# A decoder step in float32 on one core: the place of one low-part step in VectorE's order, in the odd tile of each pair

## Chip, cores and metric

One core of one Trainium2 chip runs the whole program in a single launch. The metric is the device time of one execution in microseconds (us); for the kernel before, the median of three runs is given. Profiles come from one execution that the hardware profiler recorded.

## What is computed

One layer of a hybrid decoder for two request groups that share the weights: 1024 prompt tokens and 8 x 4 sample tokens, 1056 in all, with a model width of 1024. The layer is a half-step feed-forward block, a mixer (sparse attention in three branches beside a pooling mixer) and a second half-step feed-forward block. The change lies in the feed-forward block, which the program runs twice:

```python
D_MODEL = 1024
D_FF = 2816

def swiglu_ffn(x, g, w_gate, w_up, w_down):
    h = rmsnorm(x, g)
    return (jax.nn.silu(h @ w_gate) * (h @ w_up)) @ w_down

...
        xp = xp + 0.5 * swiglu_ffn(xp, *ffn1)
        xs = xs + 0.5 * swiglu_ffn(xs, *ffn1)
        ...
        xp = xp + 0.5 * swiglu_ffn(xp, *ffn2)
        xs = xs + 0.5 * swiglu_ffn(xs, *ffn2)
```

## The kernel before

**Tiles and stages.** Each feed-forward block is one stage, `stage_ffn` (stages `f1` and `f2`; the mixer's stages lie between them). The tokens lie along the free dimension, cut into three thirds (chunks 0, 1 and 2) of 352 columns. The 2816 hidden channels are cut into 22 tiles `g` of 128 channels, and two tiles make one of 11 pairs `q`; the even tile comes first, the odd tile second. For each tile TensorE computes gate and up (`tile`), and behind the odd tile of a pair it computes the pair's down products: 24 of them, 8 blocks of output channels for each of the three thirds. `order_of(q)` says which third comes first: (1, 0, 2) in all pairs but the last of a stage, which has (0, 1, 2).

**High and low parts.** A float32 operand is split into a rounded high part and the low part that is left, and a product is three matmuls (`product3`, L110 to L114): high by high, high by low, low by high. ScalarE makes the high parts (`high_w` of the weights, L502; `high_a` of the activation, L529), VectorE the low parts (`low_w`, L630; `low_a`, L663). `a_hi` and `a_lo` hold the activation's parts for the two tiles of a pair.

**Gate and up.** A tile takes eight weight forms 0 to 7. Some are loaded halves (`gu_raw`), some are sums of halves that VectorE makes (`sum_w`, L626), as the first two thirds are computed in a Strassen-like form; the third third is computed plainly. VectorE puts the banks together (`base`, `above`, `fifth`, `far`), multiplies by the row norm (`rescale`, L654, after ScalarE's Silu, L523) and by up (`activate`, L659). The product for a third lies in `gate_of[c]`, that is `near`, `far`, `third` for c = 0, 1, 2 (`third` shows as `in_var` or `f_var` in the trace). `activate(g, c)` is followed by ScalarE's `high_a(g, c)` and then VectorE's `low_a(g, c)`, which raises `a_ready[c]`.

**Order.** Each engine's order is written out by hand, and semaphores hold the engines together. At the end of a tile VectorE runs, from `rescale(g, 1)` on (L751 to L768): the second third's product; next weights 1 (low part) and 2 (sum); the sum for the first third's up (waits for event 10, TensorE's form 7 of the first two thirds); the first third's product; the second third's low part; next weights 2 and 3; the last third's product (waits for event 11, the end of the tile on TensorE); the first third's low part; next weights 3; the last third's low part. Then come the 24 updates of the trunk (`update`, L669). ScalarE runs at the same time: next weights 0, `high_a(g, 1)`, next weights 1 and 2, `high_a(g, 0)`, next weights 3, `high_a(g, 2)` (L577 to L586).

**Down products.** TensorE waits for `a_ready[c]` at the first product of each third (L890). The products go round four banks (`down_bank`): product n of a pair goes to bank n % 4, and from n = 4 on it waits until update n - 4 has read that bank (`down_free`, L892). A product is six matmuls: two tiles of the pair, three each. `update` n waits for product n and adds half of it to the trunk.

**Loads.** SP loads the next tiles' weights in halves (`load_half`); each waits for a count of `w_lo_done`, that is for low parts of the weights that VectorE has made.

Of the kernel before, what the change touches and what calls it, by code (L numbers as in the profile page):

```python
# [116 lines left out]
def chunk(c):  # L117
    return slice(c * CH, (c + 1) * CH)
# [200 lines left out]
def stage_ffn(nc, mem, K, xT, gain, w_gate, w_up, w_down, name, b_sum, copies=(), copied=None,  # L319
# [17 lines left out]
    with ExitStack() as scope:  # L337
# [86 lines left out]
        def event(g, e):  # L424
            return EVENTS * g + e
# [11 lines left out]
        with nc.Block() as block:  # L437
# [174 lines left out]
            def _(dve):  # L612
                def sum_w(v, i):
                    gate_1, gate_2, up_1, up_2 = gu_raw[:, 0, 0:KH], gu_raw[:, 0, KH:KT], gu_raw[:, 1, 0:KH], gu_raw[:, 1, KH:KT]
                    at, count = SUM_OF[i]
                    if i != 1:
                        dve.wait_ge(raw_landed[0][i == 5], 16 * v + 16)
                    if i in (1, 2):
                        dve.wait_ge(raw_landed[1][0], 16 * v + 16)
                    if i == 1:  # L620
                        dve.wait_ge(raw_landed[1][1], 16 * v + 16)
                    if i in (3, 5):
                        dve.wait_ge(w_summed, 4 * v + count - 1)
                    a, b, op = {1: (up_1, up_2, ALU.add), 2: (up_1, gate_1, ALU.subtract),
                                3: (w_sum[:, 0], gate_1, ALU.subtract), 5: (gate_2, w_sum[:, 0], ALU.subtract)}[i]
                    dve.tensor_tensor(w_sum[:, at], a, b, op).then_inc(w_summed, 1)  # L626

                def low_w(v, i):
                    dve.wait_ge(w_hi_done, 8 * v + i + 1)
                    dve.tensor_tensor(w_lo[:, i % 4], form(i), w_hi[:, i % 4].bitcast(F32),  # L630
                                      ALU.subtract).then_inc(w_lo_done, 1)
# [20 lines left out]
                def rescale(g, c):  # L652
                    dve.wait_ge(silu_done[c], g + 1)
                    dve.tensor_tensor(gate_of[c], gate_of[c], inv[:, chunk(c)], ALU.mult).then_inc(silu_scaled[c], 1)  # L654

                def activate(g, c, up, ready, count):
                    dve.wait_ge(silu_scaled[c], g + 1)
                    dve.wait_ge(ready, count)
                    dve.tensor_tensor(gate_of[c], gate_of[c], up, ALU.mult).then_inc(act_done[c], 1)  # L659

                def low_a(g, c):
                    dve.wait_ge(a_hi_done[c], g + 1)
                    dve.tensor_tensor(a_lo[:, g % 2, chunk(c)], gate_of[c], a_hi[:, g % 2, chunk(c)].bitcast(F32),  # L663
                                      ALU.subtract).then_inc(a_ready[c], 1)

                def update(q, n):
                    c, m = order_of(q)[n // KT], n % KT
                    dve.wait_ge(down_done, DOWNS * q + n + 1)
                    dve.scalar_tensor_tensor(xT[:, m, chunk(c)], down_bank[n % 4], 0.5, xT[:, m, chunk(c)],  # L669
                                             ALU.mult, ALU.add).then_inc(down_free, 1)  # L670
                    return c, m
# [35 lines left out]
                for q in range(PAIRS):  # L707
                    for g in (2 * q, 2 * q + 1):
                        more = g + 1 < FT
                        sum_w(g, 5)  # L710
                        low_w(g, 4)
                        low_w(g, 5)
                        low_w(g, 6)
                        if g == 0:
                            norm.mean_square(dve, sum_bank, 2)
                        dve.wait_ge(product_done, event(g, 5))
                        dve.wait_ge(first_copied, g + 1)
                        dve.tensor_tensor(base, base, bank_6, ALU.add).then_inc(base_done, 1)
                        dve.wait_ge(base_done, g + 1)
                        dve.tensor_tensor(above, base, bank_7, ALU.add).then_inc(above_done, 1)  # L720
                        low_w(g, 7)
                        if g == 0:
                            dve.wait_ge(above_done, 1)
                            norm.tmp = far
                            norm.invert(dve, 2)
                        dve.wait_ge(above_done, g + 1)
                        dve.wait_ge(fifth_copied, g + 1)
                        dve.tensor_tensor(fifth, above, fifth, ALU.add).then_inc(up_far_done, 1)
                        dve.wait_ge(product_done, event(g, 6))
                        if g:  # L730
                            dve.wait_ge(a_ready[0], g)
                        dve.tensor_tensor(near, bank_1, inv[:, chunk(0)], ALU.mult).then_inc(gate_scaled[0], 1)
                        dve.wait_ge(product_done, event(g, 7))
                        if g:
                            dve.wait_ge(a_ready[2], g)
                        dve.tensor_tensor(third, bank_gate, inv[:, chunk(2)], ALU.mult).then_inc(gate_scaled[2], 1)
                        if g % 2 == 0:
                            dve.wait_ge(wd_hi_done, q + 1)
                            dve.tensor_tensor(wd_lo, wd_raw, wd_hi[:].bitcast(F32), ALU.subtract).then_inc(wd_split, 1)  # L739
                        rescale(g, 0)  # L740
                        rescale(g, 2)
                        dve.wait_ge(product_done, event(g, 8))
                        if g:
                            dve.wait_ge(a_ready[1], g)
                        dve.tensor_tensor(far, base, bank_5, ALU.add).then_inc(far_summed, 1)
                        dve.wait_ge(far_summed, g + 1)
                        dve.tensor_tensor(far, far, inv[:, chunk(1)], ALU.mult).then_inc(gate_scaled[1], 1)
                        if more:
                            sum_w(g + 1, 1)
                            low_w(g + 1, 0)  # L750
                        rescale(g, 1)  # L751
                        activate(g, 1, fifth, up_far_done, g + 1)
                        if more:
                            low_w(g + 1, 1)
                            sum_w(g + 1, 2)
                        dve.wait_ge(product_done, event(g, 10))
                        dve.wait_ge(far_summed, g + 1)
                        dve.tensor_tensor(base, base, bank_7, ALU.add).then_inc(up_near_done, 1)
                        activate(g, 0, base, up_near_done, g + 1)
                        low_a(g, 1)  # L760
                        if more:
                            low_w(g + 1, 2)
                            sum_w(g + 1, 3)
                        activate(g, 2, bank_up, product_done, event(g, 11))
                        low_a(g, 0)
                        if more:
                            low_w(g + 1, 3)
                        low_a(g, 2)  # L768
                    if q:
                        dve.wait_ge(down_free, DOWNS * q)  # L770
                    for n in range(DOWNS):
                        c, m = update(q, n)
                        if q < PAIRS - 1:
                            continue
                        if ahead:
                            if c == 1:
                                next_norm.low(dve, xT, h_hi, h_lo, 0, range(m, m + 1))
                            if c == 2 and m < LOWS_AHEAD:
                                next_norm.low(dve, xT, h_hi, h_lo, 1, range(m, m + 1))
                            if (c, m) == (2, 0):  # L780
                                next_norm.fold(dve, 0)
                            if (c, m) == (2, 5):
                                next_norm.mean_square(dve, bank_5, 0)
                        if finish:
                            if (c, m) in SQUARED_BEHIND:
                                fin.mean_square(dve, SQUARED_BEHIND[(c, m)])
                            if (c, m) in NORMED_BEHIND:
                                if (c, m) == (1, 4):
                                    dve.wait_ge(fin.gain_in, 16)
                                fin.invert_and_left(dve, NORMED_BEHIND[(c, m)])  # L790
# [2498 lines left out]
```

## Time and profile before

| | us |
|---|---|
| median of 3 runs | 2894.51 |
| lowest and highest run | 2894.26, 2901.41 |
| profiled execution | 2893.93 |
| its span, first to last instruction | 2892.3 |

In that span the stage `f1` takes about 791 us (458 to 1249) and `f2` about 777 us (2097 to 2874). How to read the rows below: times are us from the start of the span unless marked ns. PE is TensorE's matmuls, DVE is VectorE, ACT is ScalarE, L112 is line 112 of the kernel. A matmul's recorded length overlaps the next one's, so the pace of matmuls is read from start to start. The same holds for VectorE and ScalarE when they run back to back. The note in brackets at the end of a row is the idle time of that engine just before, and what ended it; "issue" means that the engine waited for nothing that the profile shows. PEclk is the clock that TensorE was granted as a share of 2.4 GHz: 1.00 is that, 0.50 is 1.2 GHz.

### The profile page before, as it was taken

What the parts mean: (1) busy time and instruction counts of PE and PEld (TensorE: products, weight loads), DVE (VectorE), ACT (ScalarE), POOL (GpSimd) and SP (SyncE); (2) the same over time, 40 slices, a digit from 0 to 9 for tenths busy, and PEclk for the clock granted to TensorE, in tenths of its full rate; (3) what the DMA queues carried; (4) which work ended last, traced back from release to release, by engine and by line L of the source; (5) the groups of instructions that cost most, each with busy time, mean ns of one, the idle gap of its engine ahead of it and who ended that gap; (6) DMA issues with size and microseconds to landing.
All of it is one profiled execution on the core that took longest, in us unless ns stands there. A gap on an engine that the chain in (4) does not pass through costs nothing. (4 is left out here: it accounts for less than half of the span.)

```text
span 2892.3 us, 44546 instructions
## 1 busy us (share of the span) xinstructions
PE 2597.1 (90%) x17112; PEld 2437.7 (84%) x17112; DVE 1761.2 (61%) x3447; ACT 1111.7 (38%) x2099; POOL 384.7 (13%) x427
## 2 busy tenths in 40 slices
PE   4999986999999999999988888677979999999997
PEld 4898885999999999988976666456879999999997
DVE  5444446766666666664147768555386666666666
ACT  4656555222222222232346656434152222222223
POOL 4444430000000000000002222451000000000001
PEclk9999998999999999999979979999999999999999
DMA  4131311311111111031311010586011111111111
GB/s 179 63 124 63 124 61 46 106 48 45 44 45 55 48 44 44 30 113 43 100 62 45 23 45 34 178 286 220 30 30 45 44 45 44 48 59 48 52 45 68
DMA packets 173315, 207.93 MB, mean 72 GB/s; under 512 B 16750, under 2 KB 154863, under 8 KB 170410
## 3 DMA queue, kind: packets, MB, share of 16 engines
q1 hardware_dynamic: 162434, 144.91, 15.9%
q0 software_dynamic: 10672, 60.19, 5.6%
q8 instruction: 137, 2.24, 0.3%
q14 instruction: 72, 0.59, 0.1%
HBM read 191.39 MB, written 18.01 MB: 72 GB/s over the span
## 5 line engine op out<-in xcount | busy, mean ns | idle before, releaser
L669 DVE SCALAR_TENSOR_TENSOR trunk<-f_bank,trunk 128x352 f32<-128x352 f32 x528 | 272.7, 523 | 198.0 <-PE f_bank L114 198.0
L112 PE MATMUL f_bank<-f_a_hi,f_wd_hi 128*128 128x352 f32 x1056 | 347.0, 329 | 44.7 <-issue 40.4
L113 PE MATMUL f_bank<-f_a_lo,f_wd_hi 128*128 128x352 f32 x1056 | 345.1, 327 | 0.0
L114 PE MATMUL f_bank<-f_a_hi,f_wd_lo 128*128 128x352 f32 x1056 | 344.4, 326 | 0.0
L112 PE MATMUL cs_sum<-cs_x_hi,cs_w_hi 128*128 128x256 f32 (+1 forms) x768 | 231.1, 301 | 32.4 <-DVE cs_x_lo L1379 22.1
L112 PEld LDWEIGHTS f_bank<-f_a_hi,f_wd_hi 128*128 128x128 f32 x1056 | 201.7, 191 | 50.4 <-issue 50.3
L112 PE MATMUL f_bank<-f_s_hi,f_w_hi 128*128 128x352 f32 x704 | 228.0, 324 | 0.0
L114 PE MATMUL f_bank<-f_s_hi,f_w_lo 128*128 128x352 f32 x704 | 227.4, 323 | 0.0
L113 PE MATMUL f_bank<-f_s_lo,f_w_hi 128*128 128x352 f32 x704 | 226.3, 321 | 0.0
L114 PE MATMUL cs_sum<-cs_x_hi,cs_w_lo 128*128 128x256 f32 (+1 forms) x768 | 218.6, 285 | 0.0
L113 PE MATMUL cs_sum<-cs_x_lo,cs_w_hi 128*128 128x256 f32 (+1 forms) x768 | 218.4, 284 | 0.0
L114 PEld LDWEIGHTS f_bank<-f_a_hi,f_wd_lo 128*128 128x128 f32 x1056 | 203.0, 192 | 0.0
L1236 POOL TENSOR_TENSOR cs_x_lo<-cs_x,cs_x_hi 128x516 fp32r<-128x516 f32 x128 | 171.0, 1336 | 234.8 <-ACT cs_x_hi L1293 234.8
L113 PEld LDWEIGHTS f_bank<-f_a_lo,f_wd_hi 128*128 128x128 f32 x1056 | 201.9, 191 | 0.1
L560 ACT ACTIVATE f_base<-f_bank 128x352 f32<-128x352 f32 x44 | 20.0, 453 | 472.7 <-PE f_bank L114 472.7
L630 DVE TENSOR_TENSOR f_w_lo<-f_gu_raw,f_w_hi 128x512 fp32r<-128x512 f32 x176 | 121.1, 688 | 119.4 <-ACT f_w_hi L502 119.1
L112 PE MATMUL f_bank<-f_h_hi,f_w_hi 128*128 128x352 f32 x528 | 171.7, 325 | 20.0 <-DVE f_h_lo L644 15.5
L112 PEld LDWEIGHTS cs_sum<-cs_x_hi,cs_w_hi 128*128 128x128 f32 x768 | 147.6, 192 | 43.1 <-DVE cs_x_lo L1379 40.3
L112 PE MATMUL f_bank<-in_h_hi,f_w_hi 128*128 128x352 f32 x528 | 171.1, 324 | 6.5 <-DVE f_w_lo L630 4.9
L114 PE MATMUL f_bank<-f_h_hi,f_w_lo 128*128 128x352 f32 x528 | 171.4, 325 | 0.0
L630 DVE TENSOR_TENSOR f_w_lo<-f_w_sum,f_w_hi 128x512 fp32r<-128x512 f32 x176 | 121.1, 688 | 82.5 <-ACT f_w_hi L502 80.2
L113 PE MATMUL f_bank<-f_h_lo,f_w_hi 128*128 128x352 f32 x528 | 171.3, 324 | 0.0
(447 smaller groups left out, 6859.7 us busy)
## 6 DMA issues: line engine op xcount, KB each, us to landing
f_gu_raw<-in_w_ffn_gate_dram SPq DMA_DIRECT2D x88, 256.0 KB, 3.0
f_gu_raw<-in_w_ffn_up_dram SPq DMA_DIRECT2D x88, 256.0 KB, 3.0
as_pages<-in_cache_kv_slc_dram SPq DMA_DIRECT2D x128, 128.0 KB, 4.0
as_pages<-in_cache_kv_slc_dram POOLq DMA_DIRECT2D x128, 128.0 KB, 4.2
at_spread<-saved_rows SPq DMA_DIRECT2D x16, 768.0 KB, 4.1
in_w_raw<-in_w_ffn_down_dram SPq DMA_DIRECT2D x11, 1024.0 KB, 5.0
f_wd_raw<-in_w_ffn_down_dram SPq DMA_DIRECT2D x11, 1024.0 KB, 5.0
x_saved<-trunk SPq DMA_DIRECT2D x2, 2112.0 KB, 13.8
```

The costliest lines, as they stand in the source:

```text
L112: pe.matmul(out, w_hi, x_hi, start=first, stop=False, skip_group_check=onto)
L113: pe.matmul(out, w_hi, x_lo, start=False, stop=False, skip_group_check=onto)
L114: return pe.matmul(out, w_lo, x_hi, start=False, stop=last, skip_group_check=onto)
L560: act.activation(base, bank_1, ACT.Copy).then_inc(first_copied, 1)
L630: dve.tensor_tensor(w_lo[:, i % 4], form(i), w_hi[:, i % 4].bitcast(F32), ALU.subtract).then_inc(w_lo_done, 1)
L669: dve.scalar_tensor_tensor(xT[:, m, chunk(c)], down_bank[n % 4], 0.5, xT[:, m, chunk(c)], ALU.mult, ALU.add).then_inc(down_free, 1)
L1236: pool.tensor_tensor(x_lo[s][:, 0:ODD], x[s][:, 0:ODD], x_hi[s][:, 0:ODD].bitcast(F32), ALU.subtract).then_inc(diff_lo_done, 1)
```

## The change

`low_a(g, 1)`, VectorE's low part of the second third's activation, is moved in odd tiles: from behind the first third's product to directly behind the second third's product, ahead of the next weights' low part 1, the sum 2, the sum for the first third's up and the first third's product. In even tiles it stays where it was. No instruction is added or taken out, and the other engines' programs are the same.

```diff
                         rescale(g, 1)
                         activate(g, 1, fifth, up_far_done, g + 1)
+                        if g % 2:
+                            low_a(g, 1)
                         if more:
                             low_w(g + 1, 1)
                             sum_w(g + 1, 2)
@@
                         activate(g, 0, base, up_near_done, g + 1)
-                        low_a(g, 1)
+                        if g % 2 == 0:
+                            low_a(g, 1)
                         if more:
                             low_w(g + 1, 2)
```

## Rows read from the trace of the kernel before

**Rows 1.** The page: TensorE's busy time, share and instructions.
```profile
PE 2597.1 (90%) x17112; PEld 2437.7 (84%) x17112; DVE 1761.2 (61%) x3447; ACT 1111.7 (38%) x2099; POOL 384.7 (13%) x427
```

**Rows 2.** Groups of TensorE's instructions: count, busy, mean ns, idle before and releasers.
```profile
L112 PE MATMUL f_bank<-f_a_hi,f_wd_hi 128*128 128x352 f32 x1056 | 347.0, 329 | 44.7 <-issue 40.4 <-DVE f_a_lo L663 4.3
```

**Rows 3.** Time line of TensorE, a pair's end near 676: start, length, instruction.
```profile
676.00 0.32 PE L114 MATMUL f_bank<-f_s_hi,f_w_lo 128*128 128x352 f32 x1
678.40 0.40 PE L112 MATMUL f_bank<-f_a_hi,f_wd_hi 128*128 128x352 f32 x1 [2.07 <-issue]
678.64 0.32 PE L113 MATMUL f_bank<-f_a_lo,f_wd_hi 128*128 128x352 f32 x1
...
682.33 0.32 PE L112 MATMUL f_bank<-f_a_hi,f_wd_hi 128*128 128x352 f32 x1
682.49 0.32 PE L113 MATMUL f_bank<-f_a_lo,f_wd_hi 128*128 128x352 f32 x1
```

**Rows 4.** Time line of VectorE there, and of the pair near 812.
```profile
673.89 0.53 DVE L659 TENSOR_TENSOR f_far<-f_far,f_fifth 128x352 f32<-128x352 f32 x1
675.50 0.69 DVE L630 TENSOR_TENSOR f_w_lo<-f_w_sum,f_w_hi 128x512 fp32r<-128x512 f32 x1 [1.08 <-ACT f_w_hi L502]
...
677.77 0.52 DVE L663 TENSOR_TENSOR f_a_lo<-f_far,f_a_hi 128x352 fp32r<-128x352 f32 x1
678.21 0.69 DVE L630 TENSOR_TENSOR f_w_lo<-f_w_sum,f_w_hi 128x512 fp32r<-128x512 f32 x1
...
681.32 1.81 DVE L669 SCALAR_TENSOR_TENSOR trunk<-f_bank,trunk 128x352 f32<-128x352 f32 x4
...
809.63 0.53 DVE L659 TENSOR_TENSOR f_far<-f_far,f_fifth 128x352 f32<-128x352 f32 x1
...
817.05 0.52 DVE L669 SCALAR_TENSOR_TENSOR trunk<-f_bank,trunk 128x352 f32<-128x352 f32 x1
```

**Rows 5.** Time line of ScalarE at the pair's end near 676.
```profile
674.45 0.50 ACT L529 ACTIVATE f_a_hi<-f_far 128x352 fp32r<-128x352 f32 x1 [1.75 <-DVE f_far L659]
674.86 0.61 ACT L502 ACTIVATE f_w_hi<-f_w_sum 128x512 fp32r<-128x512 f32 x1
...
679.53 0.63 ACT L502 ACTIVATE f_w_hi<-f_w_sum 128x512 fp32r<-128x512 f32 x1 [1.14 <-DVE f_w_sum L626]
```

**Rows 6.** Stretches behind waits: length, busy PE, PEld, DVE, ACT, POOL, PEclk, DMA.
```profile
541.20:543.20 2.00, 2.00 (x7) 2.00 (x8) 2.00 (x5) 0.95 (x2) 0.00 (x0) 0.50 0.00 0
...
2640.50:2642.50 2.00, 2.00 (x7) 2.00 (x8) 2.00 (x5) 0.98 (x2) 0.00 (x0) 0.50 0.00 0
...
678.40:680.40 2.00, 2.00 (x13) 2.00 (x13) 2.00 (x5) 0.87 (x2) 0.00 (x0) 1.00 0.02 4
...
2105.20:2107.00 1.80, 1.77 (x11) 1.80 (x12) 1.80 (x5) 0.00 (x0) 0.00 (x0) 1.00 0.00 0
...
517.50:519.50 2.00, 1.92 (x12) 1.92 (x13) 0.99 (x3) 0.94 (x2) 0.00 (x0) 1.00 0.91 293
...
1223.50:1225.50 2.00, 2.00 (x13) 2.00 (x14) 1.01 (x2) 0.00 (x0) 0.00 (x0) 1.00 0.00 0
```

**Rows 7.** Time line of TensorE, pair near 812: first and fifth down product.
```profile
814.13 0.59 PE L112 MATMUL f_bank<-f_a_hi,f_wd_hi 128*128 128x352 f32 x1 [2.07 <-issue]
...
819.61 0.32 PE L112 MATMUL f_bank<-f_a_hi,f_wd_hi 128*128 128x352 f32 x1
```

**Rows 8.** Time line of TensorE: first matmuls behind three shorter waits.
```profile
2105.23 0.40 PE L112 MATMUL f_bank<-f_h_hi,f_w_hi 128*128 128x352 f32 x1 [1.78 <-DVE f_h_lo L644]
...
517.58 0.43 PE L112 MATMUL f_bank<-in_h_hi,f_w_hi 128*128 128x352 f32 x1 [1.41 <-DVE f_w_lo L630]
...
1223.44 0.40 PE L112 MATMUL f_bank<-f_a_hi,f_wd_hi 128*128 128x352 f32 x1 [1.16 <-issue]
```

**Rows 9.** Time line of VectorE at the end of the first stage's last pair.
```profile
1220.39 0.52 DVE L758 TENSOR_TENSOR f_base<-f_base,f_bank 128x352 f32<-128x352 f32 x1 [1.14 <-PE f_bank L114]
...
1222.38 0.52 DVE L659 TENSOR_TENSOR in_var<-in_var,f_bank 128x352 f32<-128x352 f32 x1 [0.41 <-PE f_bank L114]
```

## The prediction

> **What bounds the kernel now.** I read the busy line of the page first, then the groups of TensorE's instructions, then the time lines of TensorE, VectorE and ScalarE around the end of one odd tile, and last the granted clock behind each of TensorE's waits. TensorE is busy for 90% of the span [rows 1]: whatever delays it in the two feed-forward stages delays the end. The stages are almost gapless but for one place. The group of the down products' first matmuls has 44.7 us of idle time before it, 40.4 us of that in 20 waits and 4.3 us in two more [rows 2]. That is one wait at the head of each of the 22 pairs of tiles. The 40.4 us bear the name "issue", so what ends them has to be found in the time lines.
>
> I take the pair that ends near 676 us. TensorE begins the tile's last matmul at 676.00 and the first down matmul at 678.40, with 2.07 us idle; it could have begun at 676.16, since matmuls follow each other by 0.16 there (682.33 and 682.49) [rows 3]. What does it wait for? In this pair the down products begin with the second third of the tokens, and need its low part. VectorE makes that from 677.77 to 678.29 [rows 4], and TensorE starts 0.11 us later. The other 19 pairs of this order look alike: 44.7 less the two last pairs' 1.16 [rows 8] leaves 2.12 us for each of the 20. The high part from which this low part is made had been ready since 674.45 + 0.50 = 674.95 [rows 5]; between stand two steps on the next tile's weights and two on the first third.
>
> **The change, part by part.** It takes one instruction out of its place and puts it four instructions earlier, in odd tiles alone. Nothing is added: the 0.52 us step stays, its wait on the high part moves with it, it issues no DMA, and no queue of SP or POOL is passed.
>
> *The new place.* VectorE ends the second third's product at 673.89 + 0.53 = 674.42, and then idles 1.08 us, until ScalarE hands it the next weights' high part: the next low part starts at 675.50 [rows 4], 0.03 us behind the end of ScalarE's step (674.86 + 0.61) [rows 5]. ScalarE makes the activation's high part before that, so the moved step can start at 674.95 + 0.03 = 674.98. Back to back, VectorE's starts are 0.44 us apart for a step of this size (677.77 to 678.21) [rows 4]. It is thus out of the way at 675.42, 0.08 us ahead of the step behind it. What is queued behind the moved wait is that weights' step and the whole tail; by these rows none of it is delayed. Cost at the new place: nothing, because an idle slot covers it. If the slot did not hold, the tail would start up to 0.44 us later.
>
> *The old place.* The tail behind it, from 678.21 to the first update at 681.32, has no idle time [rows 4], so it moves up by 0.44: the first update starts at 680.88. ScalarE's next weights' step in the tail idles until VectorE's sum releases it (679.53) [rows 5] and moves with it, and so does the next weights' load on SP, which waits for a low part there and is not awaited until a tile later.
>
> *Where the stall goes.* The second third's low part is there at 675.5, so TensorE runs on from 676.16 into the down products. But these have four banks, and the fifth product has to wait until VectorE's first update has emptied the first bank. Four products are 24 matmuls, 24 x 0.16 = 3.9 us: TensorE arrives at the fifth at 680.02 and the bank is not free. It starts at 680.88 + 0.52 (the update) + 0.11 (the delay seen at 678.40) = 681.51. Before, the fifth product started at 682.33 [rows 3], when its bank had been free since 681.32 + 0.52 + 0.11 = 681.95 (0.52 is the update's time at 817.05 [rows 4]). The gain is 0.82 us; the restart costs 0.08 of it, since the second matmul after a wait comes 0.24 us behind the first and not 0.16 [rows 3]. **0.74 us in a plain pair**: most of the 2.07 us is not gained but moved four products down, where some 1.3 us of idle time remains (last matmul ends about 680.18, next begins 681.51).
>
> *The clock.* In six of the 20 pairs the granted clock is about 0.5 (1.2 GHz) behind the wait, in the others 1.00 (2.4 GHz) ([rows 6]: the first and the last of the six, and one of the 14). What TensorE did before was the same: a full-speed tile and then this wait. The price: 819.61 - 814.13 = 5.48 us from the first to the fifth product [rows 7] against 682.33 - 678.40 = 3.93 [rows 3], so 1.55 us. Shorter waits have rows at the full clock behind them: 1.78, 1.41 and, in a last pair, 1.16 us [rows 6, 8]. The new wait of 1.3 us is nearest to these, so I take no fall, and keep a fall in six of 20 as the other end. In such a pair the fifth product goes from 819.61 to 817.05 - 0.44 + 0.63 = 817.24 [rows 4, 7], less 0.08: **2.29 us**.
>
> *The last pairs.* Each stage's last pair begins its down products with the first third, behind a 1.16 us wait ([rows 8] has the first stage's). There VectorE's product of the last third waits for TensorE until 1222.38, and the sum before it does so at 1220.39 [rows 9]. The moved step needs 0.03 + 0.50 + 0.03 + 0.44 = 1.00 us of the 1.14 us of idle time ahead of that sum; both waits still end with TensorE. Nothing is gained or lost.
>
> *The sum.* 14 x 0.74 + 6 x 2.29 = 10.4 + 13.7 = 24.1 us, all of it on TensorE's path. The profiled execution took 2893.93 us (span 2892.3 and 1.6 around it), the median of the runs is 0.58 above it: 2894.51 - 24.1 = **2870.4 us**.
>
> **The rivals.**
>
> *The clock still falls as often.* The wait at the fifth product comes after only 3.9 us of matmuls, and no row shows a bank wait here. Six falls at 1.55 take 9.3 us of the 24.1: 2894.5 - 14.8 = 2879.7. Against it stand the waits of 1.16 to 1.78 us without a fall.
>
> *Slower: the clock falls at the new wait in every pair.* It costs 1.55 in each of the 14 plain pairs against a gain of 0.74, and leaves 2.29 - 1.55 in the six: 14 x 0.81 - 6 x 0.74 = +6.9 us, 2901.4. It decides from the sixteenth of the 20 pairs (24.1 / 1.55 = 15.5). For it: six pairs fall already with the same wait ahead of them; against it: the 14 others don't, with a longer wait than the new one. The Trainium skill ("TensorE: Matmul & The Clock Gate", section "A second HAM failure mode: psum-queue depth-cycling") speaks for this case: a kernel that cycles through PSUM banks idles briefly between groups so often that its clock goes back and forth, and pays for that between bursts. By that rule the time would be the 2901.4; the rows so far bear it out for waits of 2.06 us and more, and for none below.
>
> *The slot does not hold.* If the step in its new place pushes the tail back by its whole 0.44 us, the first update stays at 681.32, and each of the 20 pairs loses 0.44: 24.1 - 8.8 = 15.3, 2879.2. For it: only 0.08 us of slot is left over. Against it: the sequence repeats closely, 7.42 us from this product to the first update in the pair at 812 and 7.43 in that at 676 [rows 4]. The Trainium skill (same page, section "Architectural detail: the array is 16× 32×32, not 1× 128×128") calls VectorE a strict FIFO, so a wait put ahead holds all that is behind it; the trace agrees (the weights' step at 675.50 idles for ScalarE with ready work behind it), and this rival is what that would cost.
>
> *It doesn't remove the wait.* If what ends the 2.07 us is not the low part, the time is about 2894.5. For it: the view says "issue". Against: two of the 22 waits are put down to this low part by name [rows 2], and 0.11 us lies between its end and the start.
>
> **How the numbers follow.** Forecast 2870.4: 0.72. Clock falls as before, 2879.7: 0.12. Slot lost, 2879.2: 0.08. Wait stays, 2894.5: 0.04. Slower, 2901.4: 0.04. The forecast's own range: the delay may be 0.08 instead of 0.11, the shift 0.52 instead of 0.44 and the restart free, together 0.19 x 20 = 3.8 us below; a few falls of the clock lie above. Range 2867 to 2881, which takes in the two middle rivals. About 0.3% (8.7 us) is what a measurement of this kernel can tell from no change. The first three cases are all beyond it, faster 0.92; the wait that stays and most of the slower case are within it, 0.06; slower by more needs falls and a lost slot at once, 0.02.
>
> **What would show it.** In the changed profile the idle time ahead of the group of down matmuls should fall from 44.7 to about 29 us (20 x 1.33 + 2 x 1.16), and move from the first to the fifth product. The low part should run in the slot ahead of the weights' step, which should keep its distance of 1.61 us from the second third's product, and the first update should come 6.98 and not 7.42 us behind that product. The clock should stand at 1.00 behind all 20 waits. The prediction is wrong if a new wait stands elsewhere, if the fifth product comes 8.06 us or more behind the second third's product (slot lost; 681.51 - 673.89 = 7.62 is forecast), or if rows at 0.5 of the clock remain.

## The result and the profile after

| | before | after |
|---|---|---|
| median, us | 2897.39 (4 runs, 2894.26 to 2901.41) | 2870.30 (4 runs, 2866.82 to 2873.65) |
| ratio after / before | | 0.9906, 95% interval 0.9886 to 0.9926 |
| profiled execution, us | 2893.93 | 2871.22 |
| its span, us | 2892.3 | 2869.6 |

The median of before is that of the runs made beside the changed kernel. The profiled executions differ by 22.7 us; 24.1 were forecast.

The first view is again the groups of TensorE's instructions (count, busy us, mean ns, idle us before, releasers), the group of the down products' first matmuls:

```profile
L112 PE MATMUL f_bank<-f_a_hi,f_wd_hi 128*128 128x352 f32 x1056 | 343.5, 325 | 28.2 <-DVE trunk L669 25.9 <-issue 2.3
```

Against [rows 2] the idle time went from 44.7 to 28.2 us, and it has another releaser: 25.9 us of it ends with the trunk's update, not with "issue" or the low part. The 2.3 us are the two last pairs, as before. TensorE's time line at the end of the same pair (start, length, instruction, idle time before it) shows where the wait now stands:

```profile
672.07 0.33 PE L114 MATMUL f_bank<-f_s_hi,f_w_lo 128*128 128x352 f32 x1
672.23 0.33 PE L112 MATMUL f_bank<-f_a_hi,f_wd_hi 128*128 128x352 f32 x1
...
675.93 0.32 PE L114 MATMUL f_bank<-f_a_hi,f_wd_lo 128*128 128x352 f32 x1
677.52 0.43 PE L112 MATMUL f_bank<-f_a_hi,f_wd_hi 128*128 128x352 f32 x1 [1.27 <-DVE trunk L669]
677.78 0.32 PE L113 MATMUL f_bank<-f_a_lo,f_wd_hi 128*128 128x352 f32 x1
```

The first down matmul follows the tile's last by 0.16 us: the wait of [rows 3] is gone. Four products later stands the new one, 1.27 us. VectorE's time line of that stretch:

```profile
669.96 0.53 DVE L659 TENSOR_TENSOR f_far<-f_far,f_fifth 128x352 f32<-128x352 f32 x1
671.05 0.53 DVE L663 TENSOR_TENSOR f_a_lo<-f_far,f_a_hi 128x352 fp32r<-128x352 f32 x1 [0.57 <-ACT f_a_hi L529]
671.57 0.69 DVE L630 TENSOR_TENSOR f_w_lo<-f_w_sum,f_w_hi 128x512 fp32r<-128x512 f32 x1
...
676.95 2.36 DVE L669 SCALAR_TENSOR_TENSOR trunk<-f_bank,trunk 128x352 f32<-128x352 f32 x5
```

The low part sits in the old idle slot; the weights' step behind it still comes 1.61 us after the second third's product (671.57 - 669.96; 675.50 - 673.89 in [rows 4]). The first update comes 6.99 us after that product, where it came 7.43.

Last the clock behind the new waits (stretch, length, busy us of PE, PEld, DVE, ACT, POOL, then PEclk, DMA share, GB/s): the first of the 20, the one above and the last.

```profile
543.40:545.40 2.00, 2.00 (x13) 2.00 (x14) 1.71 (x4) 0.00 (x0) 0.00 (x0) 1.00 0.00 0
677.50:679.50 2.00, 1.98 (x12) 1.98 (x13) 1.78 (x4) 0.00 (x0) 0.00 (x0) 1.00 0.00 0
...
2757.70:2759.70 2.00, 1.96 (x12) 1.96 (x13) 1.81 (x4) 0.00 (x0) 0.00 (x0) 1.00 0.00 0
```

All 20 stand at 1.00; the six falls of [rows 6] are gone.

**Where the 22.7 us came from.** The second third's product of the odd tile can serve as a mark in each pair. Its first and last row in each of the two stages (of the changed kernel also the second), of the kernel before:

```profile
536.61 0.53 DVE L659 TENSOR_TENSOR f_far<-f_far,f_fifth 128x352 f32<-128x352 f32 x1
...
1218.72 0.53 DVE L659 TENSOR_TENSOR f_far<-f_far,f_fifth 128x352 f32<-128x352 f32 x1
...
2158.90 0.53 DVE L659 TENSOR_TENSOR f_far<-f_far,f_fifth 128x352 f32<-128x352 f32 x1
...
2839.70 0.52 DVE L659 TENSOR_TENSOR f_far<-f_far,f_fifth 128x352 f32<-128x352 f32 x1
```

and of the changed kernel:

```profile
535.78 0.53 DVE L659 TENSOR_TENSOR f_far<-f_far,f_fifth 128x352 f32<-128x352 f32 x1
...
602.87 0.53 DVE L659 TENSOR_TENSOR f_far<-f_far,f_fifth 128x352 f32<-128x352 f32 x1
...
1205.51 0.53 DVE L659 TENSOR_TENSOR f_far<-f_far,f_fifth 128x352 f32<-128x352 f32 x1
...
2148.38 0.53 DVE L659 TENSOR_TENSOR f_far<-f_far,f_fifth 128x352 f32<-128x352 f32 x1
...
2815.93 0.53 DVE L659 TENSOR_TENSOR f_far<-f_far,f_fifth 128x352 f32<-128x352 f32 x1
```

Between the marks lie ten pairs' ends per stage: 682.11 us became 669.73 in the first (-12.4), 680.80 became 667.55 in the second (-13.2). That is 25.6 us in the part that the change touches. The rest of the span gave 2.9 us back: 0.8 us were gained ahead of the first mark, 2.7 lost between the stages' marks (940.18 us became 942.87) and some 1.0 behind the last one. Both losses lie in places that the change doesn't touch, the second stage's opening and its end; the last section shows them.

### The profile page after: what moved, and what is told of

It reads as the page before. It is cut to its first block and busy times, and to the rows that moved or that the text cites. A ratio compares the mean times of both kernels' runs of the same rounds, so it can differ in the third digit from the quotient of the medians.

```text
span 2869.6 us, 44546 instructions
## 1 busy us (share of the span) xinstructions
PE 2595.8 (90%) x17112; PEld 2434.0 (85%) x17112; DVE 1764.2 (61%) x3447; ACT 1112.5 (39%) x2099; POOL 385.2 (13%) x427
## 5 line engine op out<-in xcount | busy, mean ns | idle before, releaser
L112 PE MATMUL f_bank<-f_a_hi,f_wd_hi 128*128 128x352 f32 x1056 | 343.5, 325 | 28.2 <-DVE trunk L669 25.9
L113 PE MATMUL f_bank<-in_h_lo,f_w_hi 128*128 128x352 f32 x528 | 171.0, 324 | 0.0
```

Of the source, the lines that this page charges most:

```text
L112: pe.matmul(out, w_hi, x_hi, start=first, stop=False, skip_group_check=onto)
L113: pe.matmul(out, w_hi, x_lo, start=False, stop=False, skip_group_check=onto)
```

## The experiments

The theory has three parts. The low part of the second third starts the down products; the first update, with its four banks, sets the fifth product; and the clock falls only behind long waits. The rivals: the gain comes from VectorE's shorter tail alone; the updates held the pairs all along; the falls of the clock have nothing to do with the wait; the shorter tail is worth as much in even tiles. "Ten-pair sums" below are the distances between the marks above, both stages together; they and the counts of falls come from one profiled execution of each kernel. All were timed beside the kernel before, and the gains in us are the ratio's share of its median of 2898 us.

**Low part early, but behind the slot** (`e1_halfway`, against the kernel before):

```diff
                         if more:
                             low_w(g + 1, 1)
                             sum_w(g + 1, 2)
+                        if g % 2:
+                            low_a(g, 1)
                         dve.wait_ge(product_done, event(g, 10))
...
                         activate(g, 0, base, up_near_done, g + 1)
-                        low_a(g, 1)
+                        if g % 2 == 0:
+                            low_a(g, 1)
```

> The low part of the second third stands behind next weights 2, ahead of the sum for the first third's up: early enough to let TensorE start sooner, but not in VectorE's idle slot, so the first update stays 7.43 us behind the second third's product. Theory (the low part starts the down products, the first update sets the fifth, and the clock falls only behind waits of 2.06 us and more): the wait ahead of the first product shrinks to about 1.0 us, one of 0.3 to 0.5 us stands ahead of the fifth, which starts 8.0 us behind the second third's product where it was 8.44: 20 x (0.44 - 0.11) = 6.6 us, and no falls of the clock gives 9.3 more, together about 16 us faster than the kernel before. Rival, only the shorter tail of VectorE gives the gain and the clock is chance: 0 us. Rival, the falls of the clock don't depend on the wait: about 7 us faster.

Measured: 2878.13 us, ratio 0.9933 (0.9911 to 0.9956), some 19 us faster; the ten-pair sums are 17.2 us shorter. TensorE at the first and at the fifth product of the third pair:

```profile
675.54 0.40 PE L112 MATMUL f_bank<-f_a_hi,f_wd_hi 128*128 128x352 f32 x1 [1.02 <-issue]
...
680.09 0.43 PE L112 MATMUL f_bank<-f_a_hi,f_wd_hi 128*128 128x352 f32 x1 [0.45 <-DVE trunk L669]
```

VectorE's second third's product and low part there:

```profile
672.09 0.53 DVE L659 TENSOR_TENSOR f_far<-f_far,f_fifth 128x352 f32<-128x352 f32 x1
...
674.92 0.52 DVE L663 TENSOR_TENSOR f_a_lo<-f_far,f_a_hi 128x352 fp32r<-128x352 f32 x1
```

The fifth product comes 8.00 us behind the second third's product, as forecast. The tail is as long as before, yet the gain is there: the early start alone brings it, up to the point where the first update holds the fifth product. No row of the 20 pairs shows a fall of the clock: none behind 40 waits of 0.41 to 1.09 us. Both rivals fall (0 us, and about 7 us).

**The tail lengthened again by one step** (`e2_one_extra`, against the changed kernel; the extra step's result is used nowhere):

```diff
                         if g % 2 == 0:
                             low_a(g, 1)
+                        elif q < PAIRS - 1:
+                            dve.tensor_tensor(above, gate_of[1], a_hi[:, 1, chunk(1)].bitcast(F32), ALU.subtract)
```

> The changed kernel with one extra VectorE step of 0.44 us in the old place, in the 20 pairs that begin with the second third (its result is used nowhere): the early low part stays, the shorter tail is undone. Theory: the first update is 7.43 us behind the second third's product again, the fifth product 8.0 us, the wait ahead of it grows from 1.27 to about 1.71 us, and no fall of the clock stands behind it: 20 x 0.44 = 8.8 us slower than the changed kernel, about 16 us faster than the one before. Rival, VectorE's tail is not what ends the wait ahead of the fifth product: no slower than the changed kernel. Rival, the clock falls behind bank waits of this length too: up to 31 us more.

Measured: 2882.85 us, ratio 0.9959 (0.9941 to 0.9976), some 12 us faster than the kernel before; the span is 10.8 us above the changed kernel's. The fifth product comes 8.00 us behind the mark in all 20 pairs, so VectorE's tail sets it, as the theory says. But the sentence on the clock failed in the second stage. TensorE at the fifth product of a pair in each stage, and the stretches behind these waits and behind the one that follows in the second stage:

```profile
678.77 0.43 PE L112 MATMUL f_bank<-f_a_hi,f_wd_hi 128*128 128x352 f32 x1 [1.71 <-DVE trunk L669]
...
2157.42 0.53 PE L112 MATMUL f_bank<-f_a_hi,f_wd_hi 128*128 128x352 f32 x1 [1.82 <-DVE trunk L669]
```

```profile
678.80:680.80 2.00, 2.00 (x12) 2.00 (x13) 1.73 (x4) 0.00 (x0) 0.00 (x0) 1.00 0.00 0
...
2157.50:2159.50 2.00, 2.00 (x7) 2.00 (x8) 1.21 (x4) 0.00 (x0) 0.00 (x0) 0.52 0.00 0
2226.30:2228.30 2.00, 2.00 (x13) 2.00 (x14) 1.72 (x4) 0.00 (x0) 0.00 (x0) 1.00 0.04 8
```

Behind the 11 waits of 1.68 to 1.72 us there was no fall; behind the nine of 1.82 to 1.84 us there were four. That is the missing part of the forecast 16 us: the first stage's ten-pair sum is 7.9 us below the kernel before, the second's 2.3, and 4 x 1.55 = 6.2.

**And by a second step** (`e3_two_extra`, with this beside the step above, which now raises `spare_done`):

```diff
                         low_a(g, 0)
+                        if g % 2 and q < PAIRS - 1:
+                            dve.wait_ge(spare_done, q + 1)
+                            dve.tensor_tensor(above, gate_of[1], a_hi[:, 1, chunk(1)].bitcast(F32), ALU.subtract)
```

> As with one extra step, and a second extra step of 0.44 us behind the first third's low part. Theory: the fifth product starts 8.44 us behind the second third's product, where it did in the kernel before at full clock, and the wait ahead of it is about 2.15 us, as long as the wait ahead of the first product was before. If the clock falls behind waits of this length wherever they stand, some six or more of the 20 pairs show rows near 0.5 again and the time is about that of the kernel before, 0 to 5 us above it; if no pair shows a fall, a wait at the fifth product is not like a wait at the first and the time is about 7 us below it.

Measured: 2897.30 us, ratio 0.9997 (0.9985 to 1.0009): the whole gain is gone, though the down products still start without a wait. TensorE at the fifth product of the second and third pair, and the stretches behind:

```profile
615.33 0.66 PE L112 MATMUL f_bank<-f_a_hi,f_wd_hi 128*128 128x352 f32 x1 [2.15 <-DVE trunk L670]
...
684.83 0.43 PE L112 MATMUL f_bank<-f_a_hi,f_wd_hi 128*128 128x352 f32 x1 [2.15 <-DVE trunk L670]
```

```profile
615.40:617.40 2.00, 2.00 (x7) 2.00 (x8) 1.17 (x3) 0.00 (x0) 0.00 (x0) 0.50 0.00 0
684.80:686.80 2.00, 1.97 (x12) 1.97 (x13) 1.79 (x4) 0.00 (x0) 0.00 (x0) 1.00 0.00 0
```

Six of the 20 pairs show a fall again (waits of 2.11 to 2.27 us), as many as in the kernel before, though the wait stands four products later. So between these two places it is the length of the wait that matters, not the place or the releaser.

**Nothing left to wait for** (`e4_updates_in_tail`, against the changed kernel; the update loop then begins at 4 in these pairs, and its wait on `down_free` moves with the first update):

```diff
+                        early = g % 2 == 1 and q < PAIRS - 1
+                        if early:
+                            if q:
+                                dve.wait_ge(down_free, DOWNS * q)
+                            update(q, 0)
+                            update(q, 1)
                         activate(g, 2, bank_up, product_done, event(g, 11))
                         low_a(g, 0)
+                        if early:
+                            update(q, 2)
+                            update(q, 3)
                         if more:
                             low_w(g + 1, 3)
                         low_a(g, 2)
```

> The changed kernel, and in all pairs but a stage's last the first four updates run inside VectorE's tail: two ahead of the last third's product, two behind the first third's low part. Theory: nothing but the first update holds the fifth product, so its wait of 1.27 us and the restart go: 20 x 1.39 = 28 us faster than the changed kernel, about 51 us faster than the one before, and no wait of TensorE stands at a pair's end. Rival, the next wait takes its place (the first third's low part, now later, ahead of the ninth product, or a later update): less than 14 us faster than the changed kernel.

Measured: 2837.46 us, ratio 0.9798 (0.9773 to 0.9822), some 58 us faster than the kernel before; the span is 33.8 us below the changed kernel's, the ten-pair sums 30.5. It beats both kernels. The group of the down products' first matmuls, and VectorE's time line at the end of the third pair:

```profile
L112 PE MATMUL f_bank<-f_a_hi,f_wd_hi 128*128 128x352 f32 x1056 | 341.4, 323 | 2.3 <-issue 2.3
```

```profile
668.42 0.53 DVE L659 TENSOR_TENSOR f_far<-f_far,f_fifth 128x352 f32<-128x352 f32 x1
...
673.51 0.95 DVE L669 SCALAR_TENSOR_TENSOR trunk<-f_bank,trunk 128x352 f32<-128x352 f32 x2
...
675.24 0.95 DVE L669 SCALAR_TENSOR_TENSOR trunk<-f_bank,trunk 128x352 f32<-128x352 f32 x2
...
677.13 1.38 DVE L669 SCALAR_TENSOR_TENSOR trunk<-f_bank,trunk 128x352 f32<-128x352 f32 x3
```

Only the two last pairs' 2.3 us are left. The first update stands 5.09 us behind the mark, and nothing takes the place of the wait it held: the later low parts are in time for the other two thirds.

**The updates without the move** (`e6_updates_alone`: the edit above on the kernel before):

> The kernel before (low part in its old place) with the first four updates inside VectorE's tail, in all pairs but a stage's last. Theory: the wait of 2.07 us ahead of the first product is the low part's and stays, the fifth product had no wait to lose, falls of the clock come in about six of the 20 pairs as before: the time of the kernel before, within 5 us, and the 51 us that both edits gave together are not to be had from this one. Rival, the updates are what held the pairs and the move of the low part is not needed: some 25 us faster or more.

Measured: 2897.87 us, ratio 0.9995 (0.9982 to 1.0008). TensorE at the first product of the fourth pair, and VectorE's first update there:

```profile
746.71 0.40 PE L112 MATMUL f_bank<-f_a_hi,f_wd_hi 128*128 128x352 f32 x1 [2.07 <-issue]
```

```profile
748.02 0.52 DVE L669 SCALAR_TENSOR_TENSOR trunk<-f_bank,trunk 128x352 f32<-128x352 f32 x1 [0.21 <-PE f_bank L114]
```

The 2.07 us stay; the early update even has to wait for its product. The wait at the fifth product is hidden behind the one at the first: taking away what would cause it brings nothing as long as the first wait is there, and taking away the first shows it. Here eight pairs of the 20 show falls.

**Even tiles too** (`e5_even_too`, against the changed kernel):

```diff
-                        if g % 2:
-                            low_a(g, 1)
+                        low_a(g, 1)
...
-                        if g % 2 == 0:
-                            low_a(g, 1)
```

> The early place of the low part in even tiles too. Theory: only the odd tile is followed by down products, and in an even tile neither the low part nor the end of VectorE's tail is awaited by TensorE, so nothing changes against the changed kernel: a pair still takes 67.08 us in the first stage, and the time is within 3 us of the changed kernel's (23 us faster than the one before). Rival, a shorter tail of VectorE is worth its 0.44 us in every tile: 22 x 0.44 = 9.7 us faster than the changed kernel.

Measured: 2866.61 us, ratio 0.9897 (0.9879 to 0.9914), which overlaps the changed kernel's interval. An even tile's row shows the step in the slot, as in odd tiles:

```profile
652.91 0.53 DVE L663 TENSOR_TENSOR f_a_lo<-f_far,f_a_hi 128x352 fp32r<-128x352 f32 x1 [0.56 <-ACT f_a_hi L529]
```

But the ten-pair sums are 669.69 and 667.36 us, against 669.73 and 667.55: nothing is gained in the pairs. The span is 4.9 us shorter, outside them, and the last section shows the larger part of that.

## Why the prediction was right

- **What TensorE waited for.** The low part, as read from 0.11 us between its end and TensorE's start and not from the view's "issue". Shown by the halfway place: there the low part begins 2.83 us behind the mark (674.92, against 672.09) and not 3.88 (677.77 - 673.89, [rows 4]); it comes 1.05 us earlier, and the wait shrank by 1.05, from 2.07 to 1.02 us.
- **The new place costs nothing.** Shown: the weights' step kept its 1.61 us. Forecast was a start 1.09 us behind the mark (674.98 - 673.89), and it was 1.09.
- **The gain of a plain pair, forecast 0.74 us.** From mark to mark a pair without a fall took 67.87 us (809.63 - 673.89 = 135.74 over two pairs, [rows 4]) and takes 67.09 (669.96 - 602.87): 0.78. Two terms were mis-sized by hundredths, one each way, and make up the 0.04 us: the start came 0.05 us behind the update's end (676.95 + 0.52 = 677.47, then 677.52) and not 0.11, and the restart costs 0.10 (677.78 - 677.52 less 0.16) and not 0.08.
- **Most of the wait is only moved.** 1.3 us forecast, 1.27 measured. Running the updates in the tail took it away, and with it more than its idle time: 1.39 us a pair were expected and the ten-pair sums gave 30.5 / 20 = 1.5. The idle time in brackets counts from the modelled end of a matmul; from start to start the wait is 677.52 - 675.93 = 1.59 against a pace of 0.16, so 1.43, and the restart on top.
- **The clock.** No fall behind the new waits, as forecast, so 6 x 1.55 = 9.3 us of the 25.6 are the clock's. But the reason given was weaker than it looked. It rested on a row at the full clock behind 1.78 us. The run with one extra step shows that waits of 1.82 us fall in four of nine cases: one wait without a fall is one draw. What carried was the distance: 1.24 to 1.40 us in the changed kernel, with none of 20 falling, and none of 11 up to 1.72.
- **The slower rival** needed falls at the bank wait in 16 of 20 pairs; none came at this length, and six at 2.15 us. The rule of the Trainium skill that spoke for it ("TensorE: Matmul & The Clock Gate", section "A second HAM failure mode: psum-queue depth-cycling"), that waits between groups which cycle through PSUM banks make the clock go back and forth, does show here: in four pairs with one extra step and in six with two, not at all in the changed kernel. By these runs it is a matter of how long the wait is.
- **The lost slot and the wait that stays** did not come true; the rows above exclude both.
- **The total.** 25.6 us came in the pairs where 24.1 were summed; 0.8 us of the surplus is the 0.04 us of each of 20 pairs above; the rest lies in the second stage (13.2 us against 12.4 in the first) and is not broken down. Outside the pairs 2.9 us went the other way, which the sum did not foresee. The base moved too: the forecast was taken off 2894.51, and the median of the runs beside the changed kernel is 2897.39, so the medians differ by 27.1 us where 24.1 were summed. That the median hit the forecast within 0.1 us is therefore luck; what the working got right is the gain in the pairs.

## What to carry to other kernels

When a wait is taken away, work out at once what is late next on the same path: here 2.07 us of wait turned into 0.78 us of gain in a plain pair, since a bank held the fifth product 1.3 us; both waits had to go for the 58 us. An idle slot in which one engine waits for another is the cheapest place for a step whose inputs are ready. And a wait of TensorE has two prices, its length and, from some length on, which is not the same at every place, the clock behind it: shortening it can pay more than the time by which it is shortened.

## What the runs showed of the hardware

**At a pair's end the length of a wait decides whether the clock may fall, not whether it does.** Behind waits at a pair's end the clock fell in none of 40 up to 1.09 us (the halfway place), none of 40 from 1.23 to 1.40 (the changed kernel, even tiles too), none of 11 from 1.68 to 1.72, four of nine from 1.82 to 1.84 (both one extra step), and in six, six and eight of 20 from 2.06 to 2.50 (the kernel before, two extra steps, the updates alone). A fall there costs some 1.55 us, whether the wait is ahead of the first product (the 5.48 against 3.93 us of the prediction) or of the fifth. For the fifth, three marks of the run with two extra steps show it, a pair with a fall and one without:

```profile
606.89 0.53 DVE L660 TENSOR_TENSOR f_far<-f_far,f_fifth 128x352 f32<-128x352 f32 x1
...
676.39 0.53 DVE L660 TENSOR_TENSOR f_far<-f_far,f_fifth 128x352 f32<-128x352 f32 x1
...
744.33 0.53 DVE L660 TENSOR_TENSOR f_far<-f_far,f_fifth 128x352 f32<-128x352 f32 x1
```

The first distance is 69.50 us, the second 67.94.

**The same program part falls or does not.** At the second stage's opening TensorE waits 2.97 us for a low part of weights, in code that no edit touched. The changed kernel, first matmul behind the wait, and the stretches behind it:

```profile
2126.67 0.66 PE L112 MATMUL f_bank<-f_h_hi,f_w_hi 128*128 128x352 f32 x1 [2.97 <-DVE f_w_lo L630]
```

```profile
2126.70:2128.70 2.00, 2.00 (x7) 2.00 (x8) 0.88 (x3) 1.02 (x2) 0.00 (x0) 0.50 0.00 0
...
2130.70:2132.70 2.00, 2.00 (x9) 2.00 (x8) 2.00 (x5) 0.50 (x1) 0.00 (x0) 0.51 0.01 4
```

The kernel before at the same place:

```profile
2139.89 0.43 PE L112 MATMUL f_bank<-f_h_hi,f_w_hi 128*128 128x352 f32 x1 [2.98 <-DVE f_w_lo L630]
```

```profile
2139.90:2141.90 2.00, 2.00 (x12) 2.00 (x13) 0.90 (x2) 1.02 (x2) 0.00 (x0) 1.00 0.00 0
```

The changed kernel's matmuls run at the lower clock from 2126.67 to 2132.68 there: these 20 take 6.01 us, where the kernel before takes 3.31 (2139.89 to 2143.20). That is 2.7 us more, and so the whole of the 2.7 us that were lost between the stages' marks. Of the eight kernels seven have this wait, 2.97 to 3.03 us long. In four the clock fell behind it (the changed kernel, the halfway place, one extra step, the updates in the tail), in three it did not (the kernel before, two extra steps, even tiles too).

The stage's end tells the same. From its last mark to the end of the span the changed kernel takes some 1.0 us longer (53.6 us against 52.6). There TensorE transposes the output (L263); the 24 matmuls of one such stretch, with the clock in it, in the changed kernel:

```profile
2853.84 5.36 PE L263 MATMUL f_bank<-ident,trunk 128*128 128x128 f32 x24 [1.55 <-DVE f_b_sum L315]
...
2853.80:2855.80 2.00, 1.96 (x10) 1.99 (x11) 0.66 (x4) 1.10 (x3) 1.25 (x1) 0.50 0.18 72
```

and in the kernel before:

```profile
2877.64 2.81 PE L263 MATMUL f_bank<-ident,trunk 128*128 128x128 f32 x24 [1.55 <-DVE f_b_sum L315]
...
2877.60:2879.60 2.00, 1.96 (x18) 1.97 (x19) 0.67 (x4) 1.78 (x4) 1.24 (x1) 1.00 0.18 72
```

Of the other six kernels one has the fall here too (the updates in the tail, 53.2 us from the last mark to the end); the five without it take 52.5 to 52.6. The waits here are 1.55 us and, just before, 1.59, shorter than some behind which no fall came at a pair's end. So the lengths counted above hold for the pairs' ends alone. And two kernels whose edited parts are alike can differ by some us in other parts.
